# Hybrid encoder layer on one core: where the mixer splits its decay steps, who forms the first tile's mask product, and when GpSimd forms the others

## The chip, the cores and the metric

One core of one Trainium2 chip runs the whole kernel. The metric is the device time of one execution in microseconds; lower is better.

## What is computed

Two requests (512 and 1024 tokens, width 1024; in the kernel 4 and 8 tiles of 128 tokens) go through one layer. After a norm and an input projection each token takes two parallel mixers, attention over a compressed latent and a bidirectional Mamba-2 scan. Their outputs are joined and projected, and an expert-choice mixture of 16 experts follows. The change lies in the chunk part of the scan. Cut from the reference:

```python
cs = jnp.cumsum(dt * a, axis=2)
seg = cs[:, :, :, None] - cs[:, :, None, :]
decay_in = jnp.exp(jnp.where(lower, seg, -jnp.inf))
cb = jnp.einsum('bcqgn,bcsgn->bcqsg', cm, bm)
m = cb[..., None] * decay_in * dt[:, :, None]
y_diag = jnp.einsum('bcqsgr,bcsgrp->bcqgrp', m, x)
...
y_fwd = _ssd_scan(xh, dt[:, :, 0], a[0], bm, cm)
y_bwd = flip(_ssd_scan(flip(xh), flip(dt[:, :, 1]), a[1], flip(bm), flip(cm)))
```

## The kernel before

The kernel runs in stages, one after the other: input projection and scan states, the mixers (`mixers`, once for each request `r`), the output projection with the router, and the experts. The mixers stage goes from about 342 us to 900 us of the span. It is a program written out by hand: in each block every engine has its own list of steps (`first`, then `body` for each tile `g`), and semaphores tie the lists together.

`first` of request 0 builds keys and values from the latents (`keys`, L1140 to L1255), a software pipeline over 4 tiles, and runs the query path of tile 0 beside it (`front`, called through `beside` after each step `t` of the pipeline, `t` from -3 to 3). Then `body` goes over the 8 heads `h` of each tile. For each head TensorE computes scores (`scores`, L1798), VectorE takes their maximum and makes a bias of it (`tops`, L1588 and L1591), ScalarE takes the exponential (`exps`, L1479), TensorE turns the probabilities (`turn_p`, L1811), and ScalarE and VectorE copy them out (L1538, L1721). TensorE runs the scores one head ahead.

Beside the heads each tile's scan part runs, on all engines:

- `steps` (VectorE, L1599 and L1601) splits the decay steps into a high and a low part; both `terms` wait for it.
- `terms` multiply masks by steps into `decay_steps`: the forward half on VectorE (L1606, two instructions, one for each part), the backward half on GpSimd (L1423, two). TensorE's `seg` (L1850) sums them into the segment sums, and ScalarE takes their exponential (`seg_exp`, L1505).
- `spread_dt` (GpSimd, L1431) forms two products of a mask and `dt`, `cbdt` for the forward and `cbdt_b` for the backward direction, 128x1024 each. `join_dt` (VectorE, L1613) adds them, and `c_groups` (L1619 to L1623) multiplies the sum by C.B. `weights` (L1632) uses it.
- `take_off` (L1636), `add_off` (L1643), `add_skip` (L1648) and `gate` (L1653, L1655) assemble `y`; GpSimd's L1442 forms the skip product for `add_skip` and starts as soon as `gate` of the tile before is done.
- `divide` and `norm_o` (L1673) end the attention part of the tile before.

Each tile's `terms` and `spread_dt` run one tile ahead, those of tile 0 in `first`. VectorE's list ends `first` of request 0 with `steps`, both `terms`, `join_dt`, the norm of tile 1's query latent (L1572) and only then `tops` of head 0. In `body` its heads 3 and 4 hold `front` (L1135 to L1140), the first `terms` of the next tile (L1606), `norm_o`, `tops` of head 5, the copy L1721, `front` (L1583), `add_off` and `add_skip`; head 5 holds `gate`, head 6 `join_dt`. GpSimd's `body` is short:

```python
wait_apart(pool, gated, g, pool_turns)
# L1442: skip product
if after(i, more)[0]:
    terms(g + 1, 1 - j)
    spread_dt(g + 1, 1 - j)
```

`spread_dt` waits for `diag_mm` (TensorE's `diag`, L1887, in head 3) and then issues both products back to back.

Of the kernel before, what the change touches and what calls it, by code (L numbers as in the profile page):

```python
# [21 lines left out]
ALU = mybir.AluOpType  # L22
ACT = mybir.ActivationFunctionType
# [5 lines left out]
P = 128  # L29
# [3 lines left out]
NT = sum(T_OF) // P  # L33
# [95 lines left out]
def wait_apart(eng, sem, value, turns):  # L129


    eng.wait_ge(sem, value)
    eng.sem_inc(turns, 1)
# [15 lines left out]
class Core:  # L149
# [39 lines left out]
    def sem(self, name):  # L189

        if name not in self.sems:
            self.sems[name] = self.nc.alloc_semaphore(name)
        return self.sems[name]
# [949 lines left out]
def keys(core, A, r):  # L1143
# [20 lines left out]
    def load(sp):  # L1164
        first, end = TILES[1]
        sp.dma_start(wuq, io["w_uq"][0].rearrange("(k p) n -> p k n", p=P)).then_inc(sem("w_uq_in"), 16)
        sp.dma_start(A.at(A_NAT, NT, NAT - QL)[:, first:end], core.nat.rearrange("t p c -> p t c")[:, first:end, QL:NAT]
                     ).then_inc(sem("kv_in1"), 16)

    def on_act(act, beside):  # L1170
        act.wait_ge(sem(f"kv_in{r}"), 16)
# [89 lines left out]
def mixers(core, A, r):  # L1261
# [86 lines left out]
    def turn_of(g, j):  # L1348

        return (g - j) * 8  # L1350

    with nc.Block() as block:
        @block.sync
        def _(sp):
# [32 lines left out]
            def first():  # L1387
                if r:
                    sp.wait_ge(sem("kn_done"), NT)
                    sp.wait_ge(sem("ckv_normed"), NT)  # L1390
                    load_slab(0)
                else:
                    load_keys(sp)
                    load_tile(lo, 0)
                    load_tile(lo + 1, 1)

            def body(g, i, j, before, more, further):
# [18 lines left out]
        @block.gpsimd  # L1416
        def _(pool):
            def terms(g, j):

                wait_apart(pool, steps_done, g + 1, pool_turns)  # L1420
                wait_apart(pool, seg_mm, g * 2, pool_turns)
                for part, steps in enumerate((step_hi[:].bitcast(F32), step_lo[:])):
                    ins = nc.gpsimd.tensor_tensor(r_sum[:, part, 1], core.masks[:, M_GE, :].unsqueeze(1).broadcast_to([P, NS, P]),  # L1423
                                                  steps[:, j, 8:16].unsqueeze(2).broadcast_to([P, NS, P]), ALU.mult)
                ins.then_inc(terms_b, 1)

            def spread_dt(g, j):

                wait_apart(pool, diag_mm, g, pool_turns)
                for d, (out, m) in enumerate(((cbdt, M_LE), (cbdt_b, M_GE))):  # L1430
                    nc.gpsimd.tensor_tensor(out, core.masks[:, m, :].unsqueeze(1).broadcast_to([P, NS, P]),  # L1431
                                            dt[j][:, 8 * d:8 * d + 8].unsqueeze(2).broadcast_to([P, NS, P]),
                                            ALU.mult).then_inc(dt_spread, 1)

            def first():
                if not r:
                    terms(lo, 0)
                    spread_dt(lo, 0)

            def body(g, i, j, before, more, further):  # L1440
                wait_apart(pool, gated, g, pool_turns)
                nc.gpsimd.tensor_tensor(heads(y[:, 2]), heads(xnat[j]),  # L1442
                                        core.rows[:, ROW_D:ROW_D + 8].unsqueeze(2).broadcast_to([P, NS, HP]),
                                        ALU.mult).then_inc(xd_done, 1)
                if after(i, more)[0]:
                    terms(g + 1, 1 - j)
                    spread_dt(g + 1, 1 - j)
            tiles(pool, first, body, lambda g, j: None)

        @block.scalar  # L1450
        def _(act):
# [66 lines left out]
            def mix_y(g, j):  # L1518
# [2 lines left out]
                    act.wait_ge(mix_out[j], turn_of(g, j))  # L1521
                nc.scalar.activation(mix[j][:, 4:8, :].rearrange("p c t -> p (c t)"), b_y, ACT.Copy).then_inc(y_mixed, 1)

            def first():
                if r:
                    keys_act(act, None)
                else:
                    keys_act(act, lambda t: front(t + 3, lo, 0, 0))
                    front(Q_STATS, lo + 1, 1, 1)
                exps(lo, 0, 0)  # L1530

# [36 lines left out]
        def _(dve):  # L1568
# [40 lines left out]

            def join_dt(g):  # L1610

                dve.wait_ge(dt_spread, g * 2 + 2)
                nc.vector.tensor_tensor(cbdt, cbdt, cbdt_b, ALU.add).then_inc(cbdt_order, 1)  # L1613

            def c_groups(g, j):

# [66 lines left out]
            def first():  # L1683
                if r:
                    keys_dve(dve, None)
                else:
                    nc.vector.memset(ctz[0:64, 1, :], 0.0)
                    nc.vector.memset(ctz[64:128, 0, :], 0.0)
                    for d in range(2):
                        nc.vector.tensor_copy(turns_r[:, d], core.masks[:, (M_GT, M_LT)[d], :]).then_inc(steps_high, 1)  # L1690
                    keys_dve(dve, lambda t: front(t + 3, lo, 0, 0))
                    steps(lo, 0)
                    for part in range(2):
                        terms(lo, 0, part)
                    join_dt(lo)
                    front(Q_STATS, lo + 1, 1, 1)
                tops(lo, 0)

            def body(g, i, j, before, more, further):
                follows, place = after(i, more)  # L1700
# [1127 lines left out]
```

## Time and profile before

| what | value |
|---|---|
| median of 3 runs | 2991.36 us (2991.02 to 2996.1) |
| the profiled execution: its own time | 2988.47 us |
| its span | 2986.8 us |
| TensorE busy | 2739.8 us, 92% |
| VectorE busy | 2176.4 us, 73% |
| ScalarE busy | 1515.8 us, 51% |
| GpSimd busy | 233.8 us, 8% |
| mean granted TensorE clock | 0.966 |

A row of a timeline has its start in us from the span's start, its length in us, the engine, the line, the operation, the output and its inputs, shapes and a count; in brackets stands how long the engine was idle before it and what released it. In names, `banks` is PSUM, `masks` the mask tiles, `arena_attend` the shared buffer of this stage, which holds `cbdt`, `y`, the queries and the probabilities among others.

### The profile page before, as it was taken

What the parts mean: (1) busy time and instruction counts of PE and PEld (TensorE: products, weight loads), DVE (VectorE), ACT (ScalarE), POOL (GpSimd) and SP (SyncE); (2) the same over time, 40 slices, a digit from 0 to 9 for tenths busy, and PEclk for the clock granted to TensorE, in tenths of its full rate; (3) what the DMA queues carried; (4) which work ended last, traced back from release to release, by engine and by line L of the source; (5) the groups of instructions that cost most, each with busy time, mean ns of one, the idle gap of its engine ahead of it and who ended that gap; (6) DMA issues with size and microseconds to landing.
All of it is one profiled execution on the core that took longest, in us unless ns stands there. A gap on an engine that the chain in (4) does not pass through costs nothing. (4 is left out here: it accounts for less than half of the span.)

```text
span 2986.8 us, 50486 instructions
## 1 busy us (share of the span) xinstructions
PE 2739.8 (92%) x17710; PEld 2390.9 (80%) x17710; DVE 2176.4 (73%) x4135; ACT 1515.8 (51%) x2868; POOL 233.8 (8%) x204
## 2 busy tenths in 40 slices
PE   5999677899998948999999999999999999999992
PEld 4999454566666838999999999999999999999992
DVE  3565787777765478878878878778778778778773
ACT  4443344545443315555555555555555555555552
POOL 0000122121210001000000000000000000000001
PEclk8999899999999979999999999999999999999996
DMA  6221310122214437778677677677677677677655
GB/s 256 67 66 55 120 39 30 70 76 102 99 51 170 169 113 254 224 243 256 221 241 254 220 241 253 220 244 249 221 248 248 220 249 247 220 250 247 222 182 180
DMA packets 359778, 547.88 MB, mean 183 GB/s; under 512 B 14784, under 2 KB 287936, under 8 KB 359616
## 3 DMA queue, kind: packets, MB, share of 16 engines
q1 hardware_dynamic: 350720, 514.59, 50.4%
q0 software_dynamic: 8896, 31.46, 4.6%
q8 instruction: 62, 1.02, 0.1%
q14 instruction: 100, 0.82, 0.1%
HBM read 493.51 MB, written 52.49 MB: 183 GB/s over the span
## 5 line engine op out<-in xcount | busy, mean ns | idle before, releaser
L2638 PE MATMUL banks<-rowsT_parts,weights_high 128*128 128x384 f32 x4096 | 1213.2, 359 | 18.2 <-DVE hidden_parts L2560 14.3
L2639 PE MATMUL banks<-rowsT_parts,weights_low 128*128 128x192 f32 x4096 | 1028.3, 251 | 0.0
L2639 PEld LDWEIGHTS banks<-rowsT_parts,weights_low 128*128 128x128 f32 x4096 | 783.7, 191 | 22.4
L2638 PEld LDWEIGHTS banks<-rowsT_parts,weights_high 128*128 128x128 f32 x4096 | 770.5, 188 | 28.4 <-DVE hidden_parts L2560 17.1
L2497 DVE TENSOR_TENSOR weights_low<-keys_or_w_out,weights_high 128x1024 fp32r<-128x1024 f32 x512 | 603.3, 1217 | 1.4 <-ACT weights_high L2437 1.4
L2437 ACT ACTIVATE weights_high<-keys_or_w_out 128x1024 fp32r<-128x1024 f32 x512 | 523.7, 1049 | 39.6 <-PEq L2235 39.6
L2547 DVE TENSOR_TENSOR h_or_keys_or_sums<-banks,h_or_keys_or_sums 128x192 f32<-128x192 f32 x512 | 181.3, 354 | 313.8 <-ACT h_or_keys_or_sums L2463 313.8
L2651 PE MATMUL banks<-weights_high,hidden_parts 128*128 128x512 f32 x1536 | 403.9, 391 | 0.0
L2463 ACT ACTIVATE h_or_keys_or_sums<-banks 128x192 f32<-128x192 f32 x512 | 164.7, 322 | 454.8 <-PE banks L2615 333.5
L2651 PEld LDWEIGHTS banks<-weights_high,hidden_parts 128*128 128x128 f32 x1536 | 283.6, 188 | 56.0
L2497 DVE TENSOR_TENSOR weights_low<-slab_down,weights_high 128x1024 fp32r<-128x1024 f32 x256 | 311.5, 1217 | 12.5 <-issue 11.0
L2437 ACT ACTIVATE weights_high<-slab_down 128x1024 fp32r<-128x1024 f32 x256 | 262.3, 1049 | 0.2 <-DMA slab_down<-w_down 0.2
L2471 ACT ACTIVATE silu_gate<-h_or_keys_or_sums 128x192 f32<-128x192 f32 x256 | 92.5, 361 | 235.6 <-DVE h_or_keys_or_sums L2547 235.6
L2615 PE MATMUL banks<-weights_low,hidden_parts 128*64 128x512 f32 x512 | 201.1, 394 | 0.0
L2410 POOL DMA_INDIRECT residual<-weighted,rows_out x32 | 50.4, 1574 | 1670.4 <-DVE weighted L2536 1670.4
L1798 PE MATMUL banks<-keys_or_w_out,arena_attend 96*128 96x512 f32 x320 | 161.1, 610 | 6.2 <-DVE arena_attend L1721 4.3
L2651 PE MATMUL banks<-weights_low,hidden_parts 128*128 128x512 f32 x512 | 157.8, 389 | 0.0
L1538 ACT ACTIVATE arena_attend<-banks 128x512 f32<-128x512 f32 (+1 forms) x96 | 50.4, 525 | 172.6 <-PE banks L1811 172.5
L1811 PEld LDWEIGHTS banks<-masks,arena_attend 128*128 128x128 f32 x640 | 75.1, 141 | 73.3 <-ACT arena_attend L1479 39.8
L2178 PE MATMUL banks<-w_out_high,mixed_parts 128*128 128x512 f32 x384 | 127.4, 399 | 2.1 <-DVE mixed_parts L2141 1.6
L1811 PE MATMUL banks<-masks,arena_attend 128*128 128x128 f32 x640 | 101.0, 279 | 27.4 <-ACT arena_attend L1479 27.4
L1479 ACT ACTIVATE arena_attend<-banks,mix_bias 128x1024 f32<-128x1024 f32 (+1 forms) x96 | 93.0, 968 | 48.7 <-DVE mix_bias L1591 48.6
(312 smaller groups left out, 3677.7 us busy)
## 6 DMA issues: line engine op xcount, KB each, us to landing
keys_or_w_out<-w_gate SPq DMA_DIRECT2D x128, 1024.0 KB, 5.3
keys_or_w_out<-w_up SPq DMA_DIRECT2D x128, 1024.0 KB, 6.9
slab_down<-w_down SPq DMA_DIRECT2D x128, 1024.0 KB, 4.9
arena_attend<-w_ada SPq DMA_DIRECT2D x8, 2048.0 KB, 7.9
arena_attend<-ssd_tiles SPq DMA_DIRECT2D x12, 992.0 KB, 9.2
arena_inputs<-w_ada SPq DMA_DIRECT2D x4, 2048.0 KB, 12.0
ssd_tiles<-arena_inputs SPq DMA_DIRECT2D x24, 256.0 KB, 2.0
mixed<-arena_attend SPq DMA_DIRECT2D x12, 512.0 KB, 2.8
```

The source lines that it names most:

```text
L1479: nc.scalar.activation(prob[h % 2][:, 0:keys_n], core.banks[:, h % 2 * 1024:h % 2 * 1024 + keys_n], ACT.Exp, bias=bias[:, h % 2:h % 2 + 1] ...
L1798: mm = nc.tensor.matmul(core.banks[:, h % 2 * 1024 + k0:h % 2 * 1024 + k0 + 512], qT[j][0:DQK, h, :], kT[0:DQK, h, k0:k0 + 512], start=Tru ...
L1811: mm = nc.tensor.transpose((b_pT2[h % 2] if part else b_pT)[:, k * P:k * P + P], prob[h % 2][:, (part * half + k) * P:(part * half + k + 1 ...
L2178: mm = nc.tensor.matmul(core.ps[6 * j + half], a, b[:, k, cols], start=(k + n == 0), stop=(k == 7 and n == 2))
L2437: nc.scalar.activation(like(n, w_hi), unit_of(raw, n), ACT.Copy).then_inc(unit_hi, 1)
L2463: nc.scalar.activation(sums[:, kind, fc % 2], core.ps[2 * (fc % 2) + kind][:, CT:2 * CT], ACT.Copy).then_inc(low_out, 1)
L2497: nc.vector.tensor_tensor(like(n, w_lo), unit_of(raw, n), like(n, w_hi[:].bitcast(F32)), ALU.subtract).then_inc(unit_lo, 1)
L2547: nc.vector.tensor_tensor(sums[:, kind, fc % 2], core.ps[2 * (fc % 2) + kind][:, 0:CT], sums[:, kind, fc % 2], ALU.add).then_inc(sum_done, 1)
L2615: return nc.tensor.matmul(y_banks[1][0:CAP[0], cols], h_parts[:, fc, prompt_hi], w_lo[:, UNITS.index((2, fc)), cols], start=False, stop=en ...
L2638: nc.tensor.matmul(out[:, 0:2 * CT], w_hi[:, u, block], x[:, k, :], start=k == 0, stop=False)
L2639: mm = nc.tensor.matmul(out[:, 0:CT], w_lo[:, u, block], x[:, k, 0:CT], start=False, stop=k == KD - 1)
L2651: mm = nc.tensor.matmul(y_banks[b][:, cols], h_parts[:, fc, tokens], w[:, u, cols], start=step == 0 and first, stop=step == STEPS - 1 and ...
```

## The change

Three things are moved or replaced; what is computed stays the same up to rounding.

1. Tile 0: `steps` runs on VectorE beside the last two steps of the key pipeline instead of after it. The load of tile 0's scan record is issued ahead of the load of request 1's latents, no longer behind it.
2. Tile 0: GpSimd no longer forms the two products of mask and `dt`. ScalarE writes the backward product by head, 8 activations of 128x128 with a per-partition scale (`first_dt`), four after each of the key pipeline's last two steps. VectorE forms the forward product and adds in one go, 8 instructions of 128x128 (`join_first_dt`, SCALAR_TENSOR_TENSOR) in the place of `join_dt`. VectorE's `tops` of head 0 goes ahead of `terms` and of the join.
3. The other tiles: `spread_dt` takes one product. The first waits for `diag_mm` and, from tile 1's turn on, also for `norm_o` (`o_normed`); the second waits for `add_skip` (`y_order`).

```diff
 def load(sp):                                   # keys
     sp.dma_start(wuq, ...)
-    sp.dma_start(A.at(A_NAT, ...)[:, first:end], ...).then_inc(sem("kv_in1"), 16)
+    return lambda: sp.dma_start(A.at(A_NAT, ...)[:, first:end], ...).then_inc(sem("kv_in1"), 16)
...
-                    load_keys(sp)
+                    load_latents = load_keys(sp)
                     load_tile(lo, 0)
+                    load_latents()
                     load_tile(lo + 1, 1)
...
-            def spread_dt(g, j):
-                wait_apart(pool, diag_mm, g, pool_turns)
-                for d, (out, m) in enumerate(((cbdt, M_LE), (cbdt_b, M_GE))):
-                    nc.gpsimd.tensor_tensor(out, ...).then_inc(dt_spread, 1)
+            def spread_dt(g, j, d):
+                nc.gpsimd.tensor_tensor((cbdt, cbdt_b)[d], ...).then_inc(dt_spread, 1)
             def first():
                 if not r:
                     terms(lo, 0)
-                    spread_dt(lo, 0)
...
                     terms(g + 1, 1 - j)
-                    spread_dt(g + 1, 1 - j)
+                    wait_apart(pool, diag_mm, g + 1, pool_turns)
+                    if before or r:
+                        wait_apart(pool, o_normed, g, pool_turns)
+                    spread_dt(g + 1, 1 - j, 0)
+                    wait_apart(pool, y_order, g * 3 + 2, pool_turns)
+                    spread_dt(g + 1, 1 - j, 1)
...
+            def first_dt(g, j, h0):                # ScalarE
+                act.wait_ge(tile_in[j], turn_of(g, j) + 16)
+                for h in range(h0, h0 + 4):
+                    ins = nc.scalar.activation(cbdt_b[:, h, :], core.masks[:, M_GE, :], ACT.Copy, scale=dt[j][:, NS + h:NS + h + 1])
+                if h0:
+                    ins.then_inc(dt_spread, 1)
...
-                    keys_act(act, lambda t: front(t + 3, lo, 0, 0))
+                    def beside(t):
+                        front(t + 3, lo, 0, 0)
+                        if t >= 2:
+                            first_dt(lo, 0, 4 * (t - 2))
+                    keys_act(act, beside)
...
             def join_dt(g):
-                dve.wait_ge(dt_spread, g * 2 + 2)
+                dve.wait_ge(dt_spread, g * 2 + 1)
...
+            def join_first_dt(g, j):
+                dve.wait_ge(dt_spread, 1)
+                for h in range(NS):
+                    ins = nc.vector.scalar_tensor_tensor(out=cbdt[:, h, :], in0=core.masks[:, M_LE, :], scalar=dt[j][:, h:h + 1],
+                                                         in1=cbdt_b[:, h, :], op0=ALU.mult, op1=ALU.add)
+                ins.then_inc(cbdt_order, 1)
...
-                    keys_dve(dve, lambda t: front(t + 3, lo, 0, 0))
-                    steps(lo, 0)
+                    def beside(t):
+                        front(t + 3, lo, 0, 0)
+                        if t == 2:
+                            steps(lo, 0)
+                    keys_dve(dve, beside)
+                tops(lo, 0)
+                if not r:
                     for part in range(2):
                         terms(lo, 0, part)
-                    join_dt(lo)
+                    join_first_dt(lo, 0)
                     front(Q_STATS, lo + 1, 1, 1)
-                tops(lo, 0)
```

VectorE at the end of `first` of request 0, from the copy that ends the pipeline's step 2, before. L1229 copies keys, L1583 queries.

```order
L1583 COPY arena_attend<-banks 96x512 [waits q_turned]
L1229 COPY keys_or_w_out<-banks 96x4x128 [waits k_turned]
L1583 COPY arena_attend<-banks 96x512 [waits q_turned]
L1599 CAST steps_high<-arena_attend 128x16 [waits ssd_tile_in0]
L1601 TENSOR_TENSOR steps_low<-arena_attend,steps_high 128x16 [waits triangles_and_steps_high]
L1606 TENSOR_TENSOR decay_steps<-masks,steps_high 128x1024 [waits seg_mm,steps_split]
L1606 TENSOR_TENSOR decay_steps<-masks,steps_low 128x1024 [waits seg_mm,steps_split]
L1613 TENSOR_TENSOR arena_attend<-arena_attend 128x1024 [waits dt_spread]
L1572 TENSOR_SCALAR arena_attend<-h_or_keys_or_sums,mix_q_rstd 128x256 [waits q_rstd]
L1588 TENSOR_REDUCE mix_top<-banks 128x1 [waits scored]
L1591 TENSOR_SCALAR mix_bias<-mix_top 128x1 [waits topped]
```

And in the changed kernel (its lines 1598, 1603, 1606, 1614, 1616 and 1621 are the lines 1583, 1588, 1591, 1599, 1601 and 1606 of before):

```order
L1598 COPY arena_attend<-banks 96x512 [waits q_turned]
L1614 CAST steps_high<-arena_attend 128x16 [waits ssd_tile_in0]
L1616 TENSOR_TENSOR steps_low<-arena_attend,steps_high 128x16 [waits triangles_and_steps_high]
L1229 COPY keys_or_w_out<-banks 96x4x128 [waits k_turned]
L1598 COPY arena_attend<-banks 96x512 [waits q_turned]
L1603 TENSOR_REDUCE mix_top<-banks 128x1 [waits scored]
L1606 TENSOR_SCALAR mix_bias<-mix_top 128x1 [waits topped]
L1621 TENSOR_TENSOR decay_steps<-masks,steps_high 128x1024 [waits seg_mm,steps_split]
L1621 TENSOR_TENSOR decay_steps<-masks,steps_low 128x1024 [waits seg_mm,steps_split]
```

The split has moved ahead of the last key copy, and the maximum of head 0 ahead of the products; behind them stand the 8 instructions of the new join.

GpSimd from tile 0's terms to tile 1's turn, before:

```order
L1423 TENSOR_TENSOR decay_steps<-masks,steps_high 128x1024
L1423 TENSOR_TENSOR decay_steps<-masks,steps_low 128x1024
L1431 TENSOR_TENSOR arena_attend<-masks,arena_attend 128x1024 [waits diag_mm]
L1431 TENSOR_TENSOR arena_attend<-masks,arena_attend 128x1024
L1442 TENSOR_TENSOR arena_attend<-arena_attend,rows 128x512 [waits y_gated]
L1423 TENSOR_TENSOR decay_steps<-masks,steps_high 128x1024 [waits steps_split,seg_mm]
L1423 TENSOR_TENSOR decay_steps<-masks,steps_low 128x1024
```

And in the changed kernel from the same place on to the end of tile 1's turn:

```order
L1424 TENSOR_TENSOR decay_steps<-masks,steps_high 128x1024
L1424 TENSOR_TENSOR decay_steps<-masks,steps_low 128x1024
L1440 TENSOR_TENSOR arena_attend<-arena_attend,rows 128x512 [waits y_gated]
L1424 TENSOR_TENSOR decay_steps<-masks,steps_high 128x1024 [waits steps_split,seg_mm]
L1424 TENSOR_TENSOR decay_steps<-masks,steps_low 128x1024
L1430 TENSOR_TENSOR arena_attend<-masks,arena_attend 128x1024 [waits diag_mm]
L1430 TENSOR_TENSOR arena_attend<-masks,arena_attend 128x1024 [waits y_order]
L1440 TENSOR_TENSOR arena_attend<-arena_attend,rows 128x512 [waits y_gated]
L1424 TENSOR_TENSOR decay_steps<-masks,steps_high 128x1024 [waits steps_split,seg_mm]
L1424 TENSOR_TENSOR decay_steps<-masks,steps_low 128x1024
L1430 TENSOR_TENSOR arena_attend<-masks,arena_attend 128x1024 [waits diag_mm,o_normed]
L1430 TENSOR_TENSOR arena_attend<-masks,arena_attend 128x1024 [waits y_order]
```

Tile 0's pair of products is gone, so the skip product follows its terms directly, and each later pair is split by a wait for VectorE.

## Rows read from the trace of the kernel before

**Rows 1.** Waits, all engines: engine, line, releaser, us in total, times, longest.
```profile
PE banks L1811 <- ACT arena_attend L1479: 27.4, 12, 11.7
```
**Rows 2.** Timeline of TensorE around tile 0's first heads.
```profile
364.19 1.96 PE L1798 MATMUL banks<-keys_or_w_out,arena_attend 96*128 96x512 f32 x4 [1.03 <-DVE arena_attend L1583]
377.89 0.69 PE L1811 MATMUL banks<-masks,arena_attend 128*128 128x128 f32 x2 [11.74 <-ACT arena_attend L1479]
378.23 2.06 PE L1850 MATMUL banks<-decay_steps,triangles 128*128 128x512 f32 x4
...
382.64 0.63 PE L1811 MATMUL banks<-masks,arena_attend 128*128 128x128 f32 x2
```
**Rows 3.** Timeline of VectorE, the same stretch.
```profile
362.76 0.69 DVE L1229 COPY keys_or_w_out<-banks 96x512 f32<-96x512 f32 x1 [0.58 <-PE banks L1251]
...
364.16 0.18 DVE L1601 TENSOR_TENSOR steps_low<-arena_attend,steps_high 128x16 f32<-128x16 f32 x1
...
365.52 2.92 DVE L1606 TENSOR_TENSOR decay_steps<-masks,steps_low 128x1024 fp32r<-128x1024 f32 x1
373.93 2.05 DVE L1613 TENSOR_TENSOR arena_attend<-arena_attend 128x1024 f32<-128x1024 f32 x1 [5.49 <-POOL arena_attend L1431]
...
376.16 0.68 DVE L1588 TENSOR_REDUCE mix_top<-banks 128x1 f32<-128x512 f32 x1
...
377.42 1.22 DVE L1623 TENSOR_TENSOR arena_attend<-arena_attend 128x1024 f32<-128x1024 f32 x1
...
379.28 0.15 DVE L1591 TENSOR_SCALAR mix_bias<-mix_top 128x1 f32<-128x1 f32 x1
```
**Rows 4.** Timeline of GpSimd (POOL), the same stretch.
```profile
370.15 3.74 POOL L1431 TENSOR_TENSOR arena_attend<-masks,arena_attend 128x1024 f32<-128x1024 f32 x2
373.86 1.04 POOL L1442 TENSOR_TENSOR arena_attend<-arena_attend,rows 128x512 f32<-128x512 f32 x1
```
**Rows 5.** Timeline of GpSimd (POOL), tile 1's turn.
```profile
426.54 4.81 POOL L1431 TENSOR_TENSOR arena_attend<-masks,arena_attend 128x1024 f32<-128x1024 f32 x2 [1.06 <-PE banks L1887]
```
**Rows 6.** Timeline of VectorE, tile 1, heads 3 to 6.
```profile
426.68 2.92 DVE L1606 TENSOR_TENSOR decay_steps<-masks,steps_high 128x1024 fp32r<-128x1024 f32 x1
429.52 2.12 DVE L1673 TENSOR_SCALAR arena_attend<-arena_attend,mix_o_rstd 128x512 f32<-128x512 f32 x1
431.56 0.68 DVE L1588 TENSOR_REDUCE mix_top<-banks 128x1 f32<-128x512 f32 x1
...
433.27 0.68 DVE L1643 TENSOR_TENSOR arena_attend<-arena_attend 128x512 f32<-128x512 f32 x1
...
438.89 1.21 DVE L1613 TENSOR_TENSOR arena_attend<-arena_attend 128x1024 f32<-128x1024 f32 x1
```
**Rows 7.** Timeline of TensorE, head 5 of tiles 1 and 3.
```profile
433.29 0.44 PE L1811 MATMUL banks<-masks,arena_attend 128*128 128x128 f32 x2 [3.11 <-ACT arena_attend L1479]
...
500.86 0.44 PE L1811 MATMUL banks<-masks,arena_attend 128*128 128x128 f32 x2 [3.10 <-ACT arena_attend L1479]
```
**Rows 8.** Timeline of VectorE, two stretches of the input stage: SCALAR_TENSOR_TENSOR.
```profile
315.13 2.46 DVE L803 SCALAR_TENSOR_TENSOR arena_inputs<-arena_inputs,cols 128x256 f32<-128x256 f32 x6
...
335.91 5.41 DVE L872 SCALAR_TENSOR_TENSOR arena_inputs<-arena_inputs,chunk_decay 128x64 f32<-128x64 f32 x24
```
**Rows 9.** Timeline of ScalarE, key pipeline of request 0.
```profile
345.71 0.61 ACT L1468 ACTIVATE arena_attend<-banks,cols 128x128 f32<-128x128 f32 x2
...
362.76 0.59 ACT L1197 ACTIVATE keys_or_w_out<-banks 96x512 f32<-96x512 f32 x1 [1.27 <-PE banks L1251]
```
**Rows 10.** Timeline of GpSimd (POOL), tile 7's turn (request 1).
```profile
704.08 4.56 POOL L1431 TENSOR_TENSOR arena_attend<-masks,arena_attend 128x1024 f32<-128x1024 f32 x2 [1.82 <-PE banks L1887]
```
**Rows 11.** Timeline of VectorE, tile 7, head 4.
```profile
704.77 2.12 DVE L1673 TENSOR_SCALAR arena_attend<-arena_attend,mix_o_rstd 128x512 f32<-128x512 f32 x1
...
708.05 0.15 DVE L1591 TENSOR_SCALAR mix_bias<-mix_top 128x1 f32<-128x1 f32 x1
709.07 0.69 DVE L1721 COPY arena_attend<-banks 128x512 f32<-128x512 f32 x1 [0.86 <-PE banks L1811]
```

More of the change, by code:

```diff
@@ L1166, in load @@
         sp.dma_start(wuq, io["w_uq"][0].rearrange("(k p) n -> p k n", p=P)).then_inc(sem("w_uq_in"), 16)
-        sp.dma_start(A.at(A_NAT, NT, NAT - QL)[:, first:end], core.nat.rearrange("t p c -> p t c")[:, first:end, QL:NAT]
-                     ).then_inc(sem("kv_in1"), 16)
+        return lambda: sp.dma_start(A.at(A_NAT, NT, NAT - QL)[:, first:end], core.nat.rearrange("t p c -> p t c")[:, first:end, QL:NAT]
+                                    ).then_inc(sem("kv_in1"), 16)
     def on_act(act, beside):
@@ L1425, in terms @@
                 ins.then_inc(terms_b, 1)
-            def spread_dt(g, j):
-                wait_apart(pool, diag_mm, g, pool_turns)
-                for d, (out, m) in enumerate(((cbdt, M_LE), (cbdt_b, M_GE))):
-                    nc.gpsimd.tensor_tensor(out, core.masks[:, m, :].unsqueeze(1).broadcast_to([P, NS, P]),
-                                            dt[j][:, 8 * d:8 * d + 8].unsqueeze(2).broadcast_to([P, NS, P]),
-                                            ALU.mult).then_inc(dt_spread, 1)
+            def spread_dt(g, j, d):
+                nc.gpsimd.tensor_tensor((cbdt, cbdt_b)[d], core.masks[:, (M_LE, M_GE)[d], :].unsqueeze(1).broadcast_to([P, NS, P]),
+                                        dt[j][:, 8 * d:8 * d + 8].unsqueeze(2).broadcast_to([P, NS, P]),
+                                        ALU.mult).then_inc(dt_spread, 1)
             def first():
```

## The prediction

> **What bounds the kernel now.** I read the busy shares first: TensorE is busy 92% of the span, so only places where it stands still, or is slowed by others, can give time. Then the waits. The change touches only the mixers, and there the longest wait of TensorE is for ScalarE's exponential (L1479), 27.4 us in 12 waits, one of 11.7 [rows 1]. The timelines show where they lie. The 11.74 us are at the very start, between the first scores and the first turn of probabilities [rows 2]. Three of 3.1 us lie in head 5 of tiles 1, 2 and 3; the first and the last of them are shown [rows 7]. Together these four are 21.1 us. In request 1 no such wait is left: eight score tiles per head keep TensorE busy.
>
> Both kinds have the same cause behind ScalarE: VectorE is late with the maximum. In the first gap its list is `terms`, a wait of 5.49 us for GpSimd's two products, the join, a norm, and only then the maximum at 376.16 [rows 3], though the scores had been ready since about 365.2 (half of the 1.96 us for two heads from 364.19 [rows 2]). In head 5 VectorE's first product for the next tile takes 2.92 us where it takes 1.2 alone (L1613 and L1623, of the same size, take 1.21 and 1.22 [rows 3, 6]), and `norm_o` 2.12. GpSimd's two products lie across exactly these two instructions: 426.54 to 431.35 [rows 5, 6]. The pattern is that of turns. GpSimd's first product ends near 428.4, VectorE's then runs to 429.6, GpSimd's second to 431.35, and `norm_o` ends right behind it. The same alternation shows in tile 0's join, 2.05 us beside a skip product that began just before it [rows 3, 4]. So two engines that each read two SBUF operands exclude each other for a whole instruction.
>
> **The first tile.** What is new, in order of time:
>
> - The split of the decay steps on VectorE, about 0.4 us, goes into an idle 0.58 us before the last key copy [rows 3]. It costs nothing; if the gap were gone, 0.4. It ends near 362.5 instead of 364.34 (L1601 at 364.16 plus 0.18).
> - ScalarE's first four activations: 0.61 for two of that shape [rows 9], so some 1.2 us, into the 1.27 us that it idles before 362.76 [rows 9]. The other four and the query's statistics come behind the last key copy and end near 365.6, before the exponential is due at 366.1. Cover gone, the cost would be up to 1.2.
> - SP issues tile 0's load one transfer earlier, about half a microsecond, and the latents of request 1 later; those are wanted 150 us on. Nothing.
> - The maximum of head 0 runs at 365.2, the turn of probabilities follows as before by 377.89 - 376.16 = 1.73, so at 366.9 [rows 2, 3].
> - GpSimd's terms start at 362.6 and end at about 366.35 (two products alone are some 1.87 each, from 3.74 for two [rows 4]). VectorE's first term, ready at 366.05, waits for that and ends at 367.5. GpSimd's skip product (1.04 alone [rows 4]) now stands right behind its terms and takes the next turn, to 368.45; VectorE's second term ends at 369.6. TensorE's segment sum starts there, 8.6 us before 378.23 [rows 2].
> - The new join: 8 SCALAR_TENSOR_TENSOR of 128x128. Six of 128x256 take 2.46 (0.40 each in a row), 24 of 128x64 take 5.41 (0.225) [rows 8]; between them by size 0.28, so 2.25 us, bounds 1.8 and 3.2. It ends at 371.85, the norm at 372.1.
> - The two group copies and the product L1623 (1.22 [rows 3]) take some 1.6, the maximum of head 1 with its bias 0.85 (from L1623's end at 378.6 to 379.43 [rows 3]), so the bias is there at 374.55 and the exponential ends at 375.25. TensorE turns head 1's probabilities at 375.35, before at 382.64 [rows 2]: **7.3 us earlier**. From there on tile 0 runs as before, so this is the shift. The first bound is 5.5 (join at 0.40 each, 0.8 of the ScalarE cover gone); the other 8.6, the shift of the segment sum itself.
>
> **The other tiles.** Their first product now waits for `norm_o`. In tiles 1, 2 and 3 VectorE's term then takes 1.15 instead of 2.84 (start to start [rows 6]) and `norm_o` about 0.35 instead of 2.04, since nothing of GpSimd's is on its way: 3.4 us less. The maximum of head 5 runs at 428.2 instead of 431.56, and TensorE's wait of 3.1 falls to nothing, because its exponential ends before TensorE gets there at 430.2. GpSimd's first product runs from 428.3 to 430.2, beside a reduction and copies out of PSUM; `add_off`, due 1.7 us behind the start of the maximum (433.27 - 431.56 [rows 6]), may meet its end, 0.2 to 0.3. The second product starts behind `add_skip`, near 431.5, and ends near 433.4. `join_dt` wants it about 4.3 us behind `add_skip` (438.89 against 434.6, where L1643 and its successor end [rows 6]), so 2.4 us are to spare. From head 5 on VectorE has no idle time in these tiles and hands its lead on: 3.4 less 0.5 for the meetings, **2.9 a tile, 8.7 for three**. Bounds: 3.4 (no meeting), and 1.4 (VectorE's next wait takes the rest).
>
> Tile 0's turn keeps its first collision, since only `diag_mm` is asked there: nothing. In the eight tiles of request 1 `norm_o` is held up too (2.12 [rows 11]), but afterwards VectorE waits 0.86 for TensorE [rows 11], which doesn't stop: nothing, at best 0.5 a tile.
>
> **A rule to weigh.** The bias, a TENSOR_SCALAR of 128x1, now falls inside each of GpSimd's products. The trace has that case: at 708.05 it took 0.15 us and didn't wait, while GpSimd's second product lasted till 708.64 [rows 10, 11]. I take nothing for it. The Trainium skill ("SBUF — State Buffer", section "Who interferes with whom") says that copies, casts and `tensor_scalar` between SBUF operands can enter a two-port mode and then wait for GpSimd's whole instruction. By that rule the bias would wait for each product's end. `norm_o`'s 2.12 agrees with the rule, the bias of 0.15 doesn't.
>
> **The sum**: 7.3 + 8.7 = 16.0 us less. The profiled execution took 2988.5, so 2972.5 for one like it; the median of the runs shown is 2.9 above it, and against it I forecast **2975.4 us**. Later stages only start earlier, since none of their transfers is tied to a fixed time. A measurement tells about 0.2%, 6 us, from no change. This case's own range: gains of 5.5 + 4.2 to 8.6 + 10.2 + 2, so 9.7 to 20.8, hence 2970.5 to 2981.7; chance 0.72.
>
> **Rivals.**
>
> 1. The collision is only moved: the second product meets `gate` and the term of head 7, the first one `add_off`, for as long as before. For it: VectorE has no free stretch in tiles 1 to 3. Against: what follows both releases for 1.7 us reads PSUM. Then only the first tile counts, 7.3: 2984. Chance 0.09.
> 2. The first tile gives little: the eight small products and the turns with GpSimd cost more than thought (each near 0.5, two more turns of 1.9), so 2 us are left there, with 8.7: 2980.7. Chance 0.07.
> 3. The bias waits for GpSimd. Its product started some 0.1 before the maximum and lasts 1.9, the maximum takes 0.7, so each bias is 1.1 late, twice a tile: 2.9 falls to 0.7 in tiles 1 to 3, and request 1, where the maximum alone lasts 1.2 and VectorE has 0.86 to spare, loses nothing. Gain 7.3 + 2.1: 2982. Chance 0.04. (It is what the Trainium skill's "SBUF — State Buffer" would have, as above.)
> 4. The lead is lost later, at a transfer or a stage border that is late anyway, so 2991. Nothing in the mixers' waits points there. Chance 0.05.
> 5. Slower: the second product is held by `y_order` until half of VectorE's work before `join_dt` is done. If it comes late, VectorE stands at `join_dt` in head 6, with the maxima of heads 7 and 0 behind it and TensorE behind those. It decides once the product takes over 4.3 us from its release in tiles 1 to 3 (alone 1.9, the longest pair of products 4.81 for two [rows 5]), more in request 1, where the heads are longer. At 2 us more than that in all 11 turns it would cost 22 and leave the kernel 6 us slower, 2997. Chance 0.03.
>
> **How the numbers follow.** The likeliest case gives 2975.4. With the spread of the runs (5 us between the lowest and the highest) and rivals 2 and 3 within, the range is 2968 to 2983; outside are rivals 1, 4, 5 and tails of the first, about 0.2. Faster by over 0.2% (below 2985.4) hold the forecast and rivals 1 to 3: 0.92. Within 0.2%: 0.05. Slower: 0.03.
>
> **What the profile would show.** Right: TensorE's 11.7 us wait split into one of about 0.8 for the exponential and one of 2 to 3 before the segment sum; `norm_o` near 0.4 us, VectorE's term 1.2 in tiles 1 to 11; no wait of 3 us in head 5; GpSimd's products 1.9 each, apart. Wrong: `norm_o` still at 2.1; VectorE waiting for GpSimd before `join_dt`; the new join over 3.2 us; biases of over 1 us; a key copy of ScalarE late by more than 0.3; a gap at the start of request 1 that grew by what the tiles gave.

## The result, and the profile after

| | before | changed |
|---|---|---|
| median | 2991.19 us (4 runs, 2990.19 to 2996.1) | 2971.75 us (4 runs, 2968.21 to 2975.45) |
| span of the profiled execution | 2986.8 us | 2970.3 us |
| TensorE busy | 2739.8 us | 2744.9 us |
| mean granted clock | 0.966 | 0.966 |

The ratio is 0.9935, with a 95% interval from 0.9922 to 0.9948, so 19.4 us less. Five more runs of it later gave 2969.88 us against 2988.27, a ratio of 0.9938 (0.9925 to 0.9952). Forecast were 2975.4 us and a range from 2968 to 2983.

The start of tile 0, to be read against [rows 2 to 4]. TensorE in the timeline of the changed kernel (its line 1825 is 1798 of before, 1838 is 1811, 1877 is 1850):

```profile
364.42 1.95 PE L1825 MATMUL banks<-keys_or_w_out,arena_attend 96*128 96x512 f32 x4 [1.03 <-DVE arena_attend L1598]
367.31 0.44 PE L1838 MATMUL banks<-masks,arena_attend 128*128 128x128 f32 x2 [0.93 <-ACT arena_attend L1482]
369.94 2.01 PE L1877 MATMUL banks<-decay_steps,triangles 128*128 128x512 f32 x4 [2.20 <-DVE decay_steps L1621]
...
375.53 0.44 PE L1838 MATMUL banks<-masks,arena_attend 128*128 128x128 f32 x2 [1.17 <-ACT arena_attend L1482]
```

VectorE and GpSimd there:

```profile
365.56 0.69 DVE L1603 TENSOR_REDUCE mix_top<-banks 128x1 f32<-128x512 f32 x1 [1.28 <-PE banks L1825]
...
366.37 1.54 DVE L1621 TENSOR_TENSOR decay_steps<-masks,steps_high 128x1024 fp32r<-128x1024 f32 x1
367.83 2.06 DVE L1621 TENSOR_TENSOR decay_steps<-masks,steps_low 128x1024 fp32r<-128x1024 f32 x1
369.81 2.18 DVE L1634 SCALAR_TENSOR_TENSOR arena_attend<-masks,arena_attend 128x128 f32<-128x128 f32 x8
...
366.79 2.02 POOL L1440 TENSOR_TENSOR arena_attend<-arena_attend,rows 128x512 f32<-128x512 f32 x1
```

The wait of 11.74 us [rows 2] has become 0.93 for the exponential, 2.20 for VectorE's second term and 1.17 for head 1. Terms and skip product take turns as the prediction had it: the first term waits for GpSimd's term, the skip product for the first term (2.02 instead of 1.04), the second term for the skip product. Counted from TensorE's first transpose of the stage (344.10 us before, 344.15 now), head 1's turn comes 7.2 us earlier, tile 0's `diag` 7.4.

ScalarE's products in the key pipeline:

```profile
361.61 1.27 ACT L1531 ACTIVATE arena_attend<-masks,arena_attend 128x128 f32<-128x128 f32 x4
362.99 0.59 ACT L1197 ACTIVATE keys_or_w_out<-banks 96x512 f32<-96x512 f32 x1
363.49 1.27 ACT L1531 ACTIVATE arena_attend<-masks,arena_attend 128x128 f32<-128x128 f32 x4
```

Four take 1.27 us and end just before the copy of keys, which is 0.18 later by the stage's own count. Tile 1, where [rows 5, 6] had the collision (VectorE, then GpSimd):

```profile
420.37 1.22 DVE L1621 TENSOR_TENSOR decay_steps<-masks,steps_high 128x1024 fp32r<-128x1024 f32 x1
421.51 0.48 DVE L1696 TENSOR_SCALAR arena_attend<-arena_attend,mix_o_rstd 128x512 f32<-128x512 f32 x1
...
422.62 0.15 DVE L1606 TENSOR_SCALAR mix_bias<-mix_top 128x1 f32<-128x1 f32 x1
...
422.17 1.90 POOL L1430 TENSOR_TENSOR arena_attend<-masks,arena_attend 128x1024 f32<-128x1024 f32 x1 [3.00 <-DVE arena_attend L1696]
425.57 1.90 POOL L1430 TENSOR_TENSOR arena_attend<-masks,arena_attend 128x1024 f32<-128x1024 f32 x1 [1.51 <-DVE arena_attend L1671]
```

The term takes 1.22 instead of 2.92, `norm_o` 0.48 instead of 2.12, both products 1.90, and no wait of 3 us is left in head 5. One meeting is in both kernels and stays: the rope product L1135, which takes 0.28 us alone, took 1.13 before (at 424.49) and 1.14 now (at 418.19), across GpSimd's second term (417.28 to 419.18). No run here takes it away.

Then comes what the prediction didn't have. Windows of the changed kernel (stretch, length, busy us by engine, then granted clock, DMA share and GB/s):

```profile
400.00:406.00 6.00, 5.18 (x28) 3.36 (x29) 4.58 (x11) 3.42 (x11) 0.00 (x0) 0.72 0.19 81
...
462.00:470.00 8.00, 7.63 (x36) 5.39 (x37) 4.68 (x11) 4.16 (x13) 0.00 (x0) 0.57 0.60 209
...
502.00:510.00 8.00, 7.36 (x16) 3.67 (x17) 3.59 (x17) 2.82 (x11) 0.00 (x0) 0.50 0.00 0
```

TensorE's clock falls to the lower of its two levels, 1.2 GHz, at the start of tile 1's turn, at that of tile 3's, and in request 1's keys. (A granted clock of 1.00 is 2.4 GHz and 0.50 is 1.2; 0.72 is a window that was partly at each, with 0.50 in each microsecond from 401 to 404.) Before, the windows of two drops were these:

```profile
434.00:440.00 6.00, 5.92 (x36) 3.64 (x34) 5.84 (x11) 2.59 (x10) 1.04 (x1) 0.72 0.00 0
...
474.00:480.00 6.00, 5.29 (x29) 3.35 (x30) 4.80 (x11) 3.76 (x11) 0.00 (x0) 0.72 0.78 276
```

The first came while VectorE was busy 5.84 of 6 us and set the pace, and cost some 0.1 us (17.09 against 16.98 in the table below). The second lies between tiles 2 and 3 and cost 1.0 (17.26 against 16.24). A drop in a tile that VectorE paces isn't always that cheap: in two other profiles of the table the clock was low for some 7 us of tile 1, at `first_tile_only` from 428 and at `before_pad7b` from 433, and the tile took 18.03 and 18.63.

And the experts took less, though nothing in them is changed. Waits between 1140 and 2900 us, of VectorE before, then of TensorE before and after:

```profile
DVE weights_low L2497 <- issue: 11.0, 11, 1.3
...
PE banks L2638 <- DVE hidden_parts L2560: 14.3, 15, 1.5
```

```profile
PE banks L2665 <- DVE hidden_parts L2587: 7.5, 15, 0.5
```

Before, VectorE stood still 11 times, for up to 1.3 us, waiting for nothing that the profile shows, and TensorE's waits for VectorE were 6.8 us longer. In the changed kernel the row of VectorE is gone.

I measured each profile below by the same marks, all taken from the starts of TensorE's rows. "To diag 0" runs from the first transpose of keys to tile 0's `diag`. "d-y" runs from `diag` to `turn_y` in tiles 0 to 3, "y-d" from there to the next tile's `diag`, "y-K" from tile 3's `turn_y` to the last turn of request 1's keys, and "experts" is first to last row of their first product. The first transpose itself lies anywhere from 342.2 to 345.1 us, and 1 to 2 us apart in two profiles of the same kernel; the distances leave that out, the whole times don't.

```
kernel            to diag 0   d-y 0..3                  y-d 0..2            y-K     experts
before            49.11       14.94 17.09 16.98 16.98   16.24 16.24 17.26   37.20   1782.5
before, again     49.03       14.95 17.07 16.99 16.98   16.24 16.24 17.27   37.21   1783.2
changed           41.72       14.95 14.02 14.02 14.02   17.26 16.25 18.78   38.93   1777.5
changed, again    41.77       14.94 14.01 14.01 14.02   17.28 16.25 18.78   38.94   1777.0
first_tile_only   43.55       14.95 18.03 16.98 16.99   17.25 16.24 17.26   37.20   1776.5
gates_only        49.83       14.94 14.02 14.01 14.01   16.24 16.25 17.32   37.14   1783.0
tile0_skip_late   43.49       14.94 14.01 14.01 14.01   17.25 17.32 18.79   38.94   1777.7
tile0_gate        41.76       14.01 14.02 14.02 14.01   17.26 17.32 16.24   37.43   1777.9
fill_clock        43.56       14.95 14.01 14.01 14.01   16.24 16.25 16.25   36.63   1777.4
before_pad7b      49.82       14.95 18.63 17.06 17.29   16.25 16.24 16.24   37.32   1777.7
gate_norm_only    43.63       14.95 16.25 15.59 15.65   17.25 16.25 17.32   39.65   1777.8
gate_skip_only    41.74       14.95 15.34 15.35 15.34   17.29 16.24 17.32   39.37   1777.6
gate_and_fill     41.68       14.01 14.02 14.01 14.01   16.25 16.25 16.25   39.46   1776.8
```

So in the first pair of profiles the mixers gained 7.4 (first tile) + 9.0 (tiles 1 to 3), gave 2.6 back between the tiles and 1.7 in the keys, 12.1 in all, and the experts added 5.0. That makes 17.1, where the spans differ by 16.5.

### The profile page after: what moved, and what is told of

Read it like the earlier page. It is cut to its first block and busy times, and to the rows that moved or that the text cites. A ratio compares the mean times of both kernels' runs of the same rounds, so it can differ in the third digit from the quotient of the medians.

```text
span 2970.3 us, 50523 instructions
## 1 busy us (share of the span) xinstructions
PE 2744.9 (92%) x17710; PEld 2391.8 (81%) x17710; DVE 2155.6 (73%) x4142; ACT 1522.5 (51%) x2876; POOL 219.5 (7%) x202
## 5 line engine op out<-in xcount | busy, mean ns | idle before, releaser
L1603 DVE TENSOR_REDUCE mix_top<-banks 128x1 f32<-128x1024 f32 (+1 forms) x96 | 100.2, 1043 | 25.4 <-PE banks L1825 25.4
L995 PE MATMUL banks<-w_in_high,h_parts 128*128 128x512 f32 (+1 forms) x384 | 116.7, 381 | 0.0
```

The source lines that it names most:

```text
L995: mm = nc.tensor.matmul(out, a, b, start=(k == 0 and n == 0), stop=(k == KD - 1 and n == 2))
L1603: nc.vector.tensor_reduce(top[:, h % 2:h % 2 + 1], core.banks[:, h % 2 * 1024:h % 2 * 1024 + keys_n], AX_X, ALU.max).then_inc(topped, 1)
```

## The experiments

The theory: VectorE and GpSimd take turns by whole instructions, and both parts of the change remove such turns from the path; some of it is given back where the clock's drops now fall, and VectorE's place in its program gives 5 us in the experts. Rivals: the clock's losses and the experts' gain are chance, or the experts gain because they start earlier, or because of ScalarE's eight more instructions.

**The same kernels again.**

> The changed kernel once more, unaltered. In the first profile of it the mixers ended 12.0 us earlier than before (first output matmul 905.0 against 916.9 us) and the experts took some 4 us less, though their code is the same. Theory N (the experts' 4 to 5 us differ from run to run): ratio 0.9935 to 0.9960, the first output matmul again within 1 us of 905.0, the experts' length (first to last L2665, 1777.5 us) another by 1 to 5 us. Theory S (the shift of the start in time, or of code, is worth 4 to 5 us in the experts): their length again within 1 us of 1777.5. On the clock: if the drops to 1.2 GHz near 400, 462 and 498 us follow from what TensorE did before, they stand at the same places again; if not, they move.

> The kernel before, unaltered, for its profile. Theory N: its experts' length (first to last L2638, 1782.5 us in the first profile) comes out 1 to 5 us different. Theory S: again within 1 us of 1782.5. The clock drops at 434 and 474 us stand there again if they follow from TensorE's idle time.

The changed kernel: 2969.88 us, ratio 0.9938 (0.9925 to 0.9952). The table has both. Every distance comes back within 0.1 us, the clock's losses of 1.0 and 1.5 us too, and the experts differ by 0.5 and 0.7. The guess of the expectation that they differ from run to run falls: the 5 us belong to the kernel.

**The first tile alone.** GpSimd's products of the other tiles back to back behind `diag`:

```diff
                     wait_apart(pool, diag_mm, g + 1, pool_turns)
-                    if before or r:
-                        wait_apart(pool, o_normed, g, pool_turns)
                     spread_dt(g + 1, 1 - j, 0)
-                    wait_apart(pool, y_order, g * 3 + 2, pool_turns)
                     spread_dt(g + 1, 1 - j, 1)
```

> Only the first tile's part: split beside the keys, mask product by ScalarE and VectorE, maximum ahead; GpSimd's two products of the other tiles back to back behind diag as before. Sum of the prediction: 7.3 us earlier at tile 0's diag (385.9 instead of 393.2), norm_o 2.12 again, TensorE's waits of 3.1 us in head 5 of tiles 1 to 3 back, the whole 7 us below the kernel before (2984, ratio 0.9976). If the first tile's lead is lost to the clock or to waits later: under 4 us.

2977.83 us, ratio 0.9963 (0.9950 to 0.9977), 11 us less, where 7 were expected. Groups of VectorE there, and TensorE's waits from 392 to 560 us:

```profile
L1693 DVE TENSOR_SCALAR arena_attend<-arena_attend,mix_o_rstd 128x512 f32<-128x512 f32 x3 | 6.3, 2114 | 0.0
```

```profile
PE banks L1835 <- ACT arena_attend L1479: 14.4, 9, 3.1
```

`norm_o` and the waits are back as expected. Tile 0's `diag` came 5.5 us earlier, not 7.3, and 1.0 was lost again ahead of tile 1 (17.25) and 0.9 in it (18.03), to two drops of the clock, so that 3.6 are left from the first transpose to the last key. The experts took 6.0 less; that is the surplus. Together 9.6, and the spans differ by 9.3. Where the 1.8 us are missing the windows tell (this kernel, then the changed one):

```profile
374.00:380.00 6.00, 5.60 (x11) 2.72 (x11) 2.84 (x7) 2.94 (x8) 0.00 (x0) 0.50 0.06 19
```

```profile
374.00:380.00 6.00, 4.83 (x23) 2.63 (x24) 3.54 (x9) 3.52 (x9) 0.00 (x0) 1.00 0.01 1
```

The clock, low since the gap, stayed at 1.2 GHz to 380 us here and had recovered by 374 there, with the same code in this stretch. Of the nine profiles with the new first tile in the table, five reach `diag` at 41.7 and four at 43.5 us, nothing between; in the five the clock is back by 371 to 374 us, in the four only by 378 to 381. What decides between the two isn't shown: the one kernel that was profiled twice, the changed one, had 41.7 both times.

**The waits alone.** The kernel before, with `spread_dt` split and placed as in the change, the first tile as before.

> Only the waits of GpSimd's products in the other tiles; the first tile as before. Sum of the prediction: 2.9 us in each of tiles 1 to 3, so 8.7 (2982.5, ratio 0.9971), norm_o 0.48, no wait of 3.1 us in head 5. If drops of the clock, which before lay in VectorE's stretches, now fall where TensorE sets the pace (1.0 and 1.5 us in tiles 1 and 3 and 1.7 in request 1's keys in the changed kernel): 8.9 less up to 4.3, so 4.6 to 8.7. Rival, that the two parts need each other: under 3.

2982.71 us (11 runs), ratio 0.9981 (0.9972 to 0.9990), 5.6 us less. `norm_o` took 0.48; tiles 1 to 3 are 3.07, 2.97 and 2.97 us shorter from `diag` to `turn_y`, 9.0 in all, and the stretches between tiles lost nothing. Together 8.3 us from the first transpose to the last key, as the first tile was 0.7 longer here (49.83 against 49.11). In the experts nothing was gained (1783.0), though they began at 1129.2 us instead of 1137.4. The profiled execution (span 2977.7) was the second shortest: the 11 runs go from 2979.19 to 2989.65, so that 5.6 and 8.3 do not contradict each other, but this spread was not explained.

**VectorE's place in its program.** The kernel before, with one zeroing instruction cut into eight, in the stretch in which VectorE waited 5.49 us anyway:

```diff
-                    nc.vector.memset(ctz[0:64, 1, :], 0.0)
...
+                    for n in range(8):
+                        nc.vector.memset(ctz[0:64, 1, 16 * n:16 * n + 16], 0.0)
                     join_dt(lo)
```

> The kernel before, one of whose two zeroing memsets is cut into 8 of 16 columns and moved into VectorE's 5.49 us wait for GpSimd in the first tile: 7 more VectorE instructions that cost nothing there, so that VectorE's program has the changed kernel's length ahead of the experts. Six profiles so far give 1782.5 to 1783.2 us for the experts with VectorE's program as before and 1776.5 to 1777.9 with the 7 more of the changed kernel. Theory P (where VectorE's instructions lie decides on a stall of up to 1.3 us in each expert): the rows DVE weights_low <- issue go, experts 1776.5 to 1778, ratio 0.9975 to 0.9985. Theory Q (ScalarE's 8 more instructions, or the mixers' earlier end, do it): experts 1782.5 to 1783.2, the rows stay, ratio 0.9995 to 1.0005.

2983.17 us (11 runs), ratio 0.9980 (0.9971 to 0.9989). The row of VectorE's issue is gone, and TensorE's wait is that of the changed kernel:

```profile
PE banks L2639 <- DVE hidden_parts L2561: 7.4, 15, 0.5
```

The experts took 1777.7 us and began at 1137.2, as before. Theory P holds, and ScalarE and the earlier start are out: seven more VectorE instructions ahead of the loop, with nothing of the change in them, are worth 5 us. The mixers gained nothing here; from the first transpose to the last key they took 203.8 us instead of 202.0, with tile 1 at 18.63 by its drop of the clock. How the place of an instruction stops the engine (what is fetched, in what blocks) no run shows.

**The clock.** In the changed kernel TensorE repeats the last turn of head 7 five times in tiles 0 to 3, into its wait for `norm_y`:

```diff
-                    turn_p(g, h, 1)
+                    turn_p(g, h, 1, 6 if h == 7 and not r else 1)
```

> The changed kernel, in which TensorE repeats the last turn of head 7 five times in each of tiles 0 to 3 (ten more transposes, about 1.1 us, into its 1.36 us wait for norm_y; the same values again). Theory C (drops of the clock after TensorE's idle time cost 1.0 us at tile 1's start and 1.5 at tile 3's): the drops at 400 and 462 us go, diag to diag of tiles 0 to 1 and 2 to 3 is shorter by 1.0 and 1.5 us, the whole 1.5 to 3 us less. Rival (these stretches are long for another reason, or the transposes push the path): no change or up to 1 us more.

2965.33 us, ratio 0.9926 (0.9912 to 0.9939). TensorE in tile 0, and the windows that were at 0.72 and 0.57:

```profile
399.92 1.75 PE L1838 MATMUL banks<-masks,arena_attend 128*128 128x128 f32 x14 [0.88 <-ACT arena_attend L1482]
401.94 0.66 PE L1921 MATMUL banks<-masks,arena_attend 128*128 128x128 f32 x4 [0.27 <-DVE arena_attend L1683]
```

```profile
400.00:406.00 6.00, 5.73 (x46) 4.33 (x47) 5.05 (x11) 4.59 (x17) 0.00 (x0) 1.00 0.37 151
...
462.00:470.00 8.00, 7.39 (x48) 4.84 (x47) 6.91 (x16) 6.01 (x18) 0.00 (x0) 1.00 0.60 209
...
502.00:510.00 8.00, 6.46 (x29) 3.35 (x27) 5.09 (x21) 4.71 (x17) 0.00 (x0) 1.00 0.01 2
```

In these windows the clock stays at 2.4 GHz; it still falls once in the keys, from 498.5 to about 502 us, where it was low from 499 to 510 in the changed kernel. The stretches between tiles are 16.24, 16.25 and 16.25 us (17.26, 16.25 and 18.78 in the changed kernel), and the keys too are 2.3 us shorter. Work that computes nothing new, put into idle time of 1.36 us, gave 5.8 us between these marks (3.5 between the tiles, 2.3 in the keys); the first tile was the long one here (43.56), so 4.0 are left from the first transpose to the last key. Expected were 1.5 to 3 for the whole, without the keys; the median is 4.5 below the changed kernel's second one. Theory C holds for the stretches between tiles, but the wait alone does not decide: the kernels without repeats have it too and lost time to a drop in 18 of their 33 such stretches in the table, those with repeats (this one and the last) in none of 6. The Trainium skill ("TensorE: Matmul & The Clock Gate", Part 1) says that this clock follows the engine's activity; the trace agrees, by the stretch at 400 us at 0.72 without the repeats and at 1.00 with them.

**Tile 0's two leftover turns.** First the skip product behind the new join:

```diff
-                wait_apart(pool, gated, g, pool_turns)
+                if before or r:
+                    wait_apart(pool, gated, g, pool_turns)
+                else:
+                    wait_apart(pool, cbdt_order, 1, pool_turns)
```

> The changed kernel, in which GpSimd's skip product of tile 0 waits for the new join, so that it no longer stands between VectorE's two terms. If the two exclude each other for a whole instruction: the second term 1.2 us instead of 2.06, the segment sum 0.9 us earlier, the whole 0.7 to 0.9 us less than the changed kernel (ratio to the kernel before 0.993 to 0.9935, not to be told apart by time; the timeline decides). If they only slow each other: the term shorter by under 0.4.

2968.57 us, ratio 0.9931 (0.9918 to 0.9945). VectorE and GpSimd:

```profile
366.31 1.21 DVE L1624 TENSOR_TENSOR decay_steps<-masks,steps_low 128x1024 fp32r<-128x1024 f32 x1
...
370.03 0.97 DVE L1646 COPY c_groups<-arena_attend 64x128 f32<-64x128 f32 x1
...
369.79 1.12 POOL L1443 TENSOR_TENSOR arena_attend<-arena_attend,rows 128x512 f32<-128x512 f32 x1 [4.50 <-DVE arena_attend L1637]
```

The second term takes 1.21 instead of 2.06, exclusion by whole instructions again. But the skip product now met a copy of `c_groups`, 0.97 instead of 0.22, which gives most of it back, and the profile had the long first tile (43.49).

Then tile 0's first product behind VectorE's term:

```diff
                     if before or r:
                         wait_apart(pool, o_normed, g, pool_turns)
+                    else:
+                        wait_apart(pool, terms_f, 3, pool_turns)
```

> The changed kernel, in which tile 0's turn also holds GpSimd's first product back, until VectorE's first term for tile 1 is done (2.92 us there still). Exclusion: that term 1.2, the head 5 wait of TensorE in tile 0 (1.07) gone, tile 0 ends 1.0 to 1.7 us earlier; of this up to 1.0 may go to another place of the clock's drop. Whole: 0 to 1.7 below the changed kernel.

2965.58 us, ratio 0.9923 (0.9909 to 0.9936). The term and GpSimd's product:

```profile
387.76 1.22 DVE L1623 TENSOR_TENSOR decay_steps<-masks,steps_high 128x1024 fp32r<-128x1024 f32 x1
...
389.16 1.90 POOL L1430 TENSOR_TENSOR arena_attend<-masks,arena_attend 128x1024 f32<-128x1024 f32 x1 [2.59 <-DVE decay_steps L1623]
```

Tile 0 is 0.94 us shorter, just under the expected 1.0 to 1.7. Against the 16.24 us of an undisturbed stretch the clock now costs 1.1 at tile 2's start in place of 2.5 at tile 3's, and the keys are 1.5 us shorter. So 0.9 us in tile 0 moved the clock's drops to where they cost 3.0 us less. The median is 4.3 below the changed kernel's, not 0 to 1.7 as expected, and these 3.0 are most of it.

**Each of the two waits alone.**

> The changed kernel without the second wait (add_skip): GpSimd's second product follows the first. Exclusion: in tiles 1 to 3 it lies across add_off or add_skip, one of which takes up to 2.5 us instead of 0.68, so that 1.2 to 1.9 us of each tile's 3.0 are lost; turn_y to diag and diag to turn_y tell it apart from the clock. Whole: 3.5 to 6 us more than the changed kernel. If the second wait is for nothing: within 1 us of it.

2973.61 us, ratio 0.9945 (0.9932 to 0.9958). Without the second wait, in tile 1:

```profile
425.66 2.27 DVE L1670 TENSOR_TENSOR arena_attend<-arena_attend 128x512 f32<-128x512 f32 x1
...
423.12 4.26 POOL L1430 TENSOR_TENSOR arena_attend<-masks,arena_attend 128x1024 f32<-128x1024 f32 x2 [2.99 <-DVE arena_attend L1695]
```

`add_skip` takes 2.27 instead of 0.69, and the tiles lose 2.2, 1.6 and 1.6 us of their 3.0 (1.2 to 1.9 expected).

> The changed kernel without the first wait (norm_o): GpSimd's first product starts behind diag, beside VectorE's term, as before. Exclusion: the term takes 2.9 us again, norm_o 0.48, so of each tile's 3.0 us 1.7 are lost and 1.3 stay; diag to turn_y 15.7 us in tiles 1 to 3 instead of 14.0. Whole: 3.5 to 5.5 us more than the changed kernel.

2971.60 us, ratio 0.9940 (0.9927 to 0.9953). Without the first wait the term is back:

```profile
418.48 2.92 DVE L1619 TENSOR_TENSOR decay_steps<-masks,steps_high 128x1024 fp32r<-128x1024 f32 x1
```

The tiles lose 1.3 us each, not the 1.7 expected: VectorE came later to head 5, and its wait of 0.28 us for TensorE there was gone. Both waits are needed for the 3.0. In the whole time the two kernels can't be told from the changed one, 3.7 and 1.7 us above its second median, with intervals that overlap; the 3.5 us and more that were expected for `gate_skip_only` as a whole didn't come. The distances show it.

**The best version**: `tile0_gate` and `fill_clock` together.

> The changed kernel with tile 0's wait for VectorE's first term (0.9 us earlier at tile 0's end) and with TensorE's repeated transposes ahead of the wait for norm_y (no drop of the clock in tiles 0 to 3, 2.6 us, and 1.4 to 2.3 in request 1's keys). If the two add up: 4.5 to 5.5 us below the changed kernel, ratio 0.9910 to 0.9922 to the kernel before. If the earlier tile 0 makes the clock fall elsewhere: 3 to 4.5.

2963.82 us, ratio 0.9914 (0.9901 to 0.9927), the lowest median of the study. Between the tiles nothing is lost, but in the keys the clock took 39.46 us for 36.63. From the first transpose to the last key it gains 4.0 us on the changed kernel, as much as `fill_clock` alone (185.9 against 190.0 us); by time it can't be told from that one. The two did not add up here. Against `tile0_gate` the repeats gained 2.1 us between the tiles and lost 2.0 in the keys: they moved the drop. Whether repeats pay thus depends on what lies behind them.

## Why the prediction was right

- **The first tile**, 7.3 us forecast, 7.4 measured in the first pair of profiles. Its steps held: split and ScalarE's products hidden (0.2 us late, not 0), the maximum at 365.6 (365.2 forecast), two terms and a skip product in turns, the segment sum 8.3 earlier (8.6 forecast), the join 2.18 us (2.25 forecast from [rows 8]). It is 5.5 in four other kernels with the same first tile, by the clock. That this term has two values was not foreseen; the lower one equals the bound of 5.5 that I had worked out from other causes, and that is luck.
- **Tiles 1 to 3**, 2.9 a tile forecast, 3.07, 2.96 and 2.96 measured. `norm_o` took 0.39 from its start to the next one, where 0.35 was forecast (0.48 in its own row; the trace of before already had 0.48 as its shortest); the second meeting that I allowed for didn't happen, but VectorE waited 0.28 us for TensorE in head 5, and TensorE 0.81 us in head 6 for a copy of VectorE's. Without either of GpSimd's two waits 1.3 to 2.2 us of each tile's gain are lost, so the mechanism is the forecast one.
- **Request 1**: nothing forecast. From its first turn on, the changed kernel stayed 12.0 us ahead, at tile 4's `diag` (559.10 against 571.14) as at tile 11's (861.89 against 873.92). Right.
- **Rule to weigh, rival 3**: the bias of 128x1 took 0.15 us within GpSimd's product. The rival is out. The section of the Trainium skill that the prediction names ("SBUF — State Buffer", "Who interferes with whom") has `tensor_scalar` contend only "when their operands meet the conditions" of the two-port mode. The prediction left that out, so the 0.15 us speak against that reading and don't by themselves contradict the page; which condition the bias fails no run here tries.
- **Rivals 1, 2 and 5** are out: tiles 1 to 3 kept their 3.0, the join was cheap, `join_dt` never waited for GpSimd. **Rival 4**, a lead lost at a transfer or a stage border, is out as it stands, but a quarter of the lead (4.3 of 16.4 us) was lost, to the clock.
- **The step that failed** is the sentence that later stages only start earlier, with the handing on of a lead from tile to tile taken as free. Two errors of about 5 us with opposite signs hid in it. The clock took 4.3 us back (1.0, 1.5 and 1.7 more than before, in y-d and y-K of the table), and the experts gave 5 to 6 us for seven more VectorE instructions, by a stall at the loop that the prediction didn't look for. My 16.0 us stood against 16.5 in the spans of the two profiles and some 19 in the medians. That is near because the errors nearly cancel, so part of the agreement is luck.

## What to carry to other kernels

Where VectorE sets the pace, look for GpSimd instructions that overlap its larger ones between SBUF tiles (products, joins, `norm_o`), and hold GpSimd back until VectorE turns to work out of PSUM: here the same instructions then cost 3 us less a tile, with no arithmetic removed. Compare distances between fixed marks in the trace instead of whole times, since drops of TensorE's clock and the place of a loop in an engine's program each move a few microseconds for reasons outside the change. Where TensorE must wait a little in front of a stretch that it paces, harmless repeats of its last instruction may keep the clock up and pay for themselves; here they did in one of two kernels, so the stretch behind has to be measured too.

## What the runs showed that I had not expected

- Seven more VectorE instructions ahead of the experts' loop shorten it by 5 us (1777.7 against 1782.5 and 1783.2), and a stall of up to 1.3 us marked "issue" that came 11 times is gone.
- The clock's drops recur in the same places in a second execution of the same kernel (17.26 and 17.27 before tile 3 in the kernel before, 18.78 twice in the changed one). After the first gap the clock recovers at one of two times, 1.8 us apart in effect, in kernels with the same first tile; what decides isn't shown.
- A VectorE copy of 64x128 between SBUF tiles waited for GpSimd (0.97 against 0.22 us), while a TENSOR_SCALAR of 128x1 within GpSimd's product did not (0.15).
